# Decode attention: which half of the steps release their page gathers from inside the scoring

## The reference, cut to what matters

```
def one_seq(args):                                   # for each of 8 sequences
    pt, ql, qr, cn, kn = args                        # pt: 32 page numbers
    ckv = concat([cache_ckv[layer, pt].reshape(past, KV_LORA), cn])    # (4096 + 8, 256)
    kr  = concat([cache_kr [layer, pt].reshape(past, ROPE_DIM), kn])   # (4096 + 8, 32)
    return _latent_attention(ql[None], qr[None], ckv[None], kr[None], q_pos, k_pos)[0]

scores = (einsum("bqhc,btc->bhqt", q_lat, ckv) + einsum("bqhr,btr->bhqt", q_rope, kr)) * MLA_SCALE
p = softmax(where(k_pos <= q_pos, scores, NEG_INF));  out = einsum("bhqt,btc->bqhc", p, ckv)
```

## Time and profile before

| | |
|---|---|
| median of 3 runs | 1444.89 us (1439.93 to 1448.80) |
| the profiled execution's own time | 1448.23 us |
| its span, first to last instruction | 1446.4 us |
| mean granted TensorE clock over the span | 0.977 |
| busy: TensorE / VectorE / ScalarE / GpSimd | 96% / 59% / 36% / 17% |

### The profile page before, as it was taken

The page is one execution under the profiler, slowest core; times in us unless marked ns, Lnnn a source line. Parts: engine busy times, 40 slices in busy tenths (PEclk is TensorE's granted clock), DMA queues, the critical chain, the costliest instruction groups (busy, mean ns, idle before and its releaser), DMA issues.

```text
span 1446.4 us, 27840 instructions
## 1 busy us (share of the span) xinstructions
PE 1384.1 (96%) x11072; PEld 1206.7 (83%) x11072; DVE 853.3 (59%) x1672; ACT 519.1 (36%) x1105; POOL 247.6 (17%) x193
## 2 busy tenths in 40 slices
PE   7999989999988999898999999999999999999997
PEld 7999977766655555565999999999999999999885
DVE  3385368887666445545585676654444445567745
ACT  4221456665452222234424333443333342113100
POOL 3110037774632334410100000000000000000000
PEclk9999989999999779999999999999999999999999
DMA  6643020001463445649313112123333237452722
GB/s 231 199 154 97 1 88 1 1 1 66 145 218 104 149 140 180 217 138 383 119 45 90 45 45 89 50 85 106 98 99 121 91 98 268 167 197 74 263 88 73
DMA packets 108437, 174.36 MB, mean 121 GB/s; under 512 B 14002, under 2 KB 77298, under 8 KB 107028
## 3 DMA queue, kind: packets, MB, share of 16 engines
q1 hardware_dynamic: 98068, 136.92, 28.8%
q0 software_dynamic: 10240, 35.66, 7.2%
HBM read 138.49 MB, written 34.06 MB: 119 GB/s over the span
## 4 chain that ended last, share of the span: by engine, by line
PE 52%; DVE 0%; issue 0%; ACT 0%; DVEq 0%
PE ps L2498 35%; PE ps L2529 10%; PE ps L2563 6%; PE ps L2549 0%; DVE p_h L2871 0%; DVE p_h L2874 0%; DVE p_stats L2858 0%; DVE p_h L2854 0%; PE ps L2539 0%; DVE p_mv L2865 0%; ACT p_rt L2646 0%; DVE p_rs L2869 0%; DVE p_stats L2863 0%; DVE p_stats L2862 0%; DVE p_ve L2867 0%
## 5 line engine op out<-in xcount | busy, mean ns | idle before, releaser
L2498 PE MATMUL ps<-p_x,p_w 128*128 128x272 f32 x4032 | 506.7, 289 | 1.1 <-PEq L2029 0.7
L2498 PEld LDWEIGHTS ps<-p_x,p_w 128*128 128x128 f32 x4032 | 506.3, 188 | 1.4 <-issue 1.4
L2529 PE MATMUL ps<-p_uh,p_w 128*128 128x352 f32 (+1 forms) x576 | 141.9, 327 | 0.0
L1023 POOL TENSOR_SCALAR p_pr<-p_pr,p_rec 128x896 f32<-128x896 f32 (+3 forms) x64 | 112.3, 1764 | 134.4 <-DVE p_rec L987 134.1
L2748 DVE TENSOR_TENSOR p_w<-p_sum,p_w 128x512 fp32r<-128x512 f32 x94 | 65.0, 691 | 117.8 <-ACT p_w L1956 117.7
L1571 PE MATMUL ps<-p_kT,p_q_rows 32*64 32x256 f32 x2048 | 106.0, 463 | 24.3 <-issue 19.8
L1571 PEld LDWEIGHTS ps<-p_kT,p_q_rows 32*64 32x64 f32 x2048 | 64.2, 160 | 61.0 <-issue 55.4
L1956 ACT ACTIVATE p_w<-p_wr 128x512 fp32r<-128x512 f32 x96 | 60.1, 626 | 131.4 <-PE ps L2529 76.0
L1068 DVE STREAM_TRANSPOSE p_kT<-p_rawc 128x1024 f32<-128x1024 f32 x64 | 77.6, 1232 | 42.7 <-DMA p_rawc<-cache_ckv,p_rows 37.5
L2529 PEld LDWEIGHTS ps<-p_uh,p_w 128*128 128x128 f32 x576 | 101.8, 188 | 0.0
L2529 PE MATMUL ps<-p_ul,p_w 128*128 128x352 f32 (+1 forms) x288 | 94.3, 328 | 0.0
(11 more groups left out here) (340 smaller groups left out, 2472.8 us busy)
## 6 DMA issues: line engine op xcount, KB each, us to landing
p_wr<-w_in SPq DMA_DIRECT2D x48, 512.0 KB, 3.6
g_kept<-p_slots SPq DMA_DIRECT2D x48, 272.0 KB, 2.5
p_ring<-g_kept SPq DMA_DIRECT2D x16, 544.0 KB, 5.3
p_x<-x_kept SPq DMA_DIRECT2D x6, 1088.0 KB, 7.2
t_kept<-p_t_raw SPq DMA_DIRECT2D x16, 272.0 KB, 2.4
p_x<-t_kept SPq DMA_DIRECT2D x4, 1088.0 KB, 9.1
p_gy<-g_kept SPq DMA_DIRECT2D x8, 544.0 KB, 6.0
p_xs<-x_prompt SPq DMA_DIRECT2D x8, 512.0 KB, 4.4
```

The source lines that it names most:

```text
L1023: nc.gpsimd.tensor_scalar(pr[:, n % PR, 0:w], pr[:, n % PR, 0:w], rec[:, n % PR:n % PR + 1], None, ALU.mult).then_inc(normed, 1)
L2498: last = pe.matmul(ps[:, lo + z, 0:PW], w[:, q % NW, part, t, :], v[:, t, z * PW:(z + 1) * PW], start=(i in STARTS and t == 0 and n == 0), ...
L2529: last = pe.matmul(ps[:, BANK_OF[g % 8], 0:tn], w[:, q % NW, part, t, :], v[:, t0:t0 + tn], start=(t == 0 and z == 0), stop=(t == KH - 1 a ...
```

## The change

A new semaphore, `mostly_scored`, is raised by the last matmul of sub-block 4 of every scoring, that is after five of the eight sub-blocks. GpSimd's latent gathers of the unbroken steps wait for it in place of `scored`. Those of the broken steps still wait for `scored`. Nothing else changes; lines behind the new one are three further down at most.

```diff
--- before.py
+++ after.py
@@ -1508,6 +1508,7 @@
         p_turned, pt_done, pv_done = sem("p_turned"), sem("pt_done"), sem("pv_done")
         o_normed, o_turned, o_placed = sem("o_normed"), sem("o_turned"), sem("o_placed")
         y_done, q6_clear = sem("y_done"), sem("q6_clear")
+        mostly_scored = sem("mostly_scored")
         block = c.enter_context(nc.Block())
 
         item = lambda b, g: b * (G + 1) + g
@@ -1568,9 +1569,11 @@
                     for f in range(2):
                         for i in range(4):
                             rows = slice(32 * i, 32 * (i + 1))
-                            pe.matmul(cols(i, f), q_rows[rows, b % 2, d, :],
+                            last = pe.matmul(cols(i, f), q_rows[rows, b % 2, d, :],
                                              kT[rows, x:x + S, 2 * f:2 * f + 2, d, :], start=(d == 0), stop=False,
                                              tile_position=(32 * i, f * R))
+                    if d == NB - 4:
+                        last.then_inc(mostly_scored, 1)
                 if NB - 1 not in part:
                     return
                 for f in range(2):
@@ -1840,7 +1843,7 @@
             for n in range(-S, NG, S):
                 for x in range(n + G, n + G + S):
                     if NAT <= x < NG:
-                        pool.wait_ge(scored, n // S + 1)
+                        pool.wait_ge(mostly_scored if n % G else scored, n // S + 1)
                         pool.wait_ge(pv_done, x - NAT + 1)
                         gather_pages(nc, a, e, x)
                 for x in range(n + AHEAD + S, n + AHEAD + 2 * S, 2):
```

## The result

The changed kernel takes **1421.98 us** (1421.17 to 1424.76, six runs), the kernel before in the same runs 1442.39 (1439.93 to 1448.80): a ratio of 0.9849, 95% interval 0.9828 to 0.9870, 20.4 us less. The forecast was 1437, so the gain is two and a half times the 8 us forecast, and the time lies just outside the range's lower end. The profiled execution took 1422.14 us with a span of 1420.3.

The account below looks back on a forecast made before the run. TensorE, kept from being fed by rows of gathers, was taken to set the decode stage's pace. 4 × 1.7 + 2 × 0 = 7 us plus about 1 for half clock took 1448.2 to 1440, so median 1437; range 1422 to 1450.

Parts of the forecast that it names:

- The hold: Decode stage: each indirect gather keeps TensorE from being fed for 1.42 us, six for 8.5; some 64 queued records run meanwhile.
- By these rows it hardly waits: Unbroken steps: the fourth gather's wait for first values, met at 494.7, ends before its turn at 495.1.
- more comes back: Rival, chance 0.17: the hold always splits and broken steps' half-clock stretch falls to 3.4 us; 18 us gained, 1427.
- the case with two pieces: If the fourth gather slips, TensorE's queue fills up between two pieces of the hold: 1.6 to 2.9 us a step gained.
- About 1 for half-clock stretches: Decode stage: TensorE's half-clock stretches get shorter, worth about 1 us in the whole sum.
- One run of gathers: Six gathers in one run hold until 499.6; 0.9 to 2.6 us a step gained, taken as 1.7, in four steps.
- The values aren't disturbed: If the hold splits, unbroken steps' values run undisturbed and the next scoring's first half ends between 501.7 and 503.
- at most about 3 us of a step can be had: Turn behind the broken scoring's first half: ScalarE's exponentials, following its finish at 499.74, cap the gain of a step.
- The signs: Changed profile: first gather 2 to 3.7 us before the scoring's last record, 64 to 70 records held; longer unbroken scorings mean wrong.
- What is late next, and the latents: ScalarE's exponentials come next behind the first half; VectorE's wait for latents gets 2 to 3 us shorter and buys nothing.
- It is the bytes: Rival, chance 0.08: transfers, not issuing of gathers, disturb TensorE; the stall moves 2.9 us forward, 17 us gained, 1428.
- Slower: Rival, chance 0.09: TensorE's queue is nearly empty at the new release and the scoring's tail is held; 15 us lost, 1460.

Follow-up runs that it names:

- the kernel without the pause: Changed kernel with both rotary gathers put before the fourth latent gather in unbroken steps: 1437.55 us, ratio 0.9932, on a chip with the hold.
- the two small gathers: Changed kernel plus two unread 64 KB gathers behind those of six broken steps: 1446.69 us, 0.9999 of before, on a chip with the hold.
- the first experiment: Changed kernel with the old release, the fourth gather of unbroken steps waiting for all four values of its step: 1423.21 us, 0.9838, with the hold.
- after three sub-blocks: Changed kernel with the release after three of eight sub-blocks in place of five: 1438.04 us, ratio 0.9949.
- the kernel with three pieces: Old release, the six gathers of unbroken steps cut into three pieces by waits for values: ratio 1.0005, only on a chip without the hold.
- the early release in all steps: Changed kernel with the release after five sub-blocks in broken steps as well: 1414.80 us, 0.9799, with the hold; 1378.51 us, 0.9934, without.
- split_only: The kernel of the first experiment, old release with a pause before the fourth gather: 1387.33 us, 0.9998 of before, on a chip without the hold.

## Why the prediction was wrong

Two steps failed: the fourth gather's wait, which was taken for met, and the half-clock term, which was taken for 1 us.

**The hold, right.** 1.42 us for each gather, whatever its size: 8 gathers hold 11.4 us. That some 64 queued records cover it is borne out as well: 67 to 72 in the long holds, 68 in the one of eight, 106 to 112 where it is filled twice. The Trainium skill gives TensorE's queue a depth of 64 ("TensorE: Matmul & The Clock Gate", Architectural detail: the array is 16× 32×32). The number is near, but the agreement is weaker than the prediction has it: beside the 71 matmul records of the hold at 478.96 stand 69 weight loads, so it holds only if the two together are one entry, and no run shows what an entry is. The Trainium skill's rule that the sides of SBUF "can't contend with each other" ("Trainium Architecture — The Big Picture", What this means for kernel authors) isn't tested here: no run shows that the hold arises at SBUF.

**"By these rows it hardly waits", wrong.** This is the step that failed first. The prediction set the end of the first values, 494.7, against the fourth gather's turn at 495.1, and left out the 1.2 us from a release to its gather that it had read itself: with it the gather comes near 495.9, and there is a pause already by the rows of before. It is longer for two more reasons. The semaphore events in the changed kernel's trace show both. The first values end 3.1 to 5.7 us behind the first gather (the prediction had 3.6), over 4 us in three of the six steps. And their signal comes out 0.4 to 1.3 us behind that end in five steps, at 4.4 to 4.6 us, when the piece of three is over; outside gathers a signal of TensorE comes 0.01 us behind its record (the median of 61, at most 0.09). The fourth gather starts 0.94 us behind the signal in all six. The prediction allowed for a late signal, by ScalarE's finish at 499.74, but only as a slip "by up to a microsecond or so" that its sum left out. So "more comes back" happened, and its chance of 0.17 was too low.

**The price of a split, too low.** Even the case with two pieces was put at 1.6 to 2.9 us a step in four steps, and at 0 in the two at full clock (12 and 52). Measured from one unbroken scoring to the next, the six pairs gave 4.3, 4.9, 4.1, 4.1, 2.8 and 4.5 us, those of 12 and 52 as much as the others.

**"About 1 for half-clock stretches", the term that was mis-sized.** In its place stand some 17 to 19 us of the 26.0. In the broken steps TensorE had 37.5 us at half clock before and has none now; half of that, if TensorE was never idle in it, is 18.8. In the step shown, the clock fell to 0.50 at 501.21, inside the hold of 8.52 us and behind its gaps, and stayed there for 10.2 us, over the turn and the second half; behind two holds of 4.26 us without long gaps it doesn't fall. The stretches with no gather about show the loss by themselves: in six steps the second halves to the values take 8.7 us less, the turns 4.7, and the rest of the first halves behind the hold 3.2, together 16.6. What is left, 7 to 9 us, are the shorter gaps less the slower values, and the 1.4 us ahead of the first changed step.

**One run of gathers, right by luck.** With one run the forecast was 8 us, and the kernel without the pause is 8.8 under before. But it has five gathers and one in place of six, and its parts are not those of the sum: its unbroken values take 48.1 us in six steps against 21.6, its first halves 22.6 against 51.6. The values stop at the sixteenth, for ScalarE's copy, which the sum didn't have.

**"The values aren't disturbed" if it splits, wrong in part.** They take 4.9 us more over six steps; 2.7 us of waits there are put down to ScalarE's copies, which wait for TensorE's late signals. And **"at most about 3 us of a step can be had"** was too strict: the finish that it starts from came late because the last value's signal did, 2.3 us behind its record, at 499.72. A step pair gave (26.0 − 1.4)/6 = 4.1 us.

**The signs.** The first gather was to start 2 to 3.7 us ahead of the scoring's last record. It does so in the step shown (3.75); in the other five it is 1.2 to 1.4. The unbroken scorings, of which longer ones were to be a sign of being wrong, are 1.7 us longer in six steps to the first value, 0.6 us to their own last record.

**What is late next, and the latents.** VectorE's wait fell from 37.5 to 11.6 us and bought nothing where gathers hold: with the wait at 40.2 us the first experiment is as fast. **It is the bytes** fell with the two small gathers. **Slower** did not come true at five sub-blocks; after three sub-blocks its mechanism shows, 16.6 us more in the unbroken scorings.

Left open: why gathers hold TensorE on some chips and not on others; what TensorE lacks in a hold; how short a row of gathers is best where they hold, since the kernel with three pieces was not run there; what of the further gain of the early release in all steps is the pause and what the release; and why some of TensorE's signals wait in a hold and others don't.

## What to carry to other kernels

Where an engine is fed from a queue and something keeps it from being fed, count the interruptions in a row and not their sum: two of 4.3 us, with time between to fill the queue, cost far less than one of 8.5 us. Look at what the engine's clock does behind the gap before costing the gap by its length; by the estimates above it was worth more here than the gap. And before crediting a change to what its diff says, run the kernel that has only its side effect: a wait that had slept in the fourth gather did the work.

## What was not expected of the hardware

- Gathers hold TensorE on three of the five chips (before at 1445.0 to 1446.9 us) and not on two (1387 us): an unbroken scoring takes 4.6 us there with gathers about, against 7.8 to 9.4 in before. Nearly all of the difference lies in the decode stage: 234.7 us in the profile of before, 175.2 in the profile of `split_only` on the other kind of chip, where it is as fast as before; the two profiled executions differ by 60.0.
- TensorE's signals come late in a hold. In the changed kernel the signal of the whole scoring comes 2.8 us behind its record in five of six steps, at the end of the piece, and the gather that waits for a value starts 1.0 to 1.24 us behind such an end, in five steps of the changed kernel, in `split_only` (490.87 behind 489.84) and after five gathers (588.64 behind 587.4). But it is not every signal, nor always the end: in the hold at 494.03 of before the values' signals come 0.81, 2.06, 3.53 and 5.69 us behind the first gather for records that end at 0.78, 1.65, 2.51 and 3.37, and in the broken steps that of the transposes 2.8 us into a hold is on time. In `split_only` on a chip without the hold no signal of scores, transposes or values is more than 0.1 us late.
- Gathers interrupt by their number: eight of them for 11.4 us, four of the eight with nothing but 64 KB each.
